# Loading the routing stage's first data during sliding attention, and attention in half blocks

## The reference

```python
def sb_attend(q, k, v, q_pos, k_pos):                      # stick-breaking attention, 8 heads x 64
    z = einsum(q, k) / 8
    mask = k_pos[None, :] < q_pos[:, None]
    log_rest = where(mask, log_sigmoid(-z), 0.0)
    suffix = cumsum(log_rest, axis=3, reverse=True) - log_rest
    a = where(mask, exp(log_sigmoid(z) + suffix), 0.0)
    return einsum(a, v)

def reference(...):
    xn = rmsnorm(x, norm1_g)
    qa, ka, va, qb, kb, vb, ga, gb = split(xn @ w_in)      # 4352 columns
    oa = sb_attend(qa, ka, va)
    ob = sliding_window_attention(qb, kb, vb)              # window 128, sinks, relative bias
    x = x + (sigmoid(ga) * (oa @ w_oa) + sigmoid(gb) * (ob @ w_ob)) @ w_o
    x = x + peer(rmsnorm(x, norm2_g))                      # 8 heads: top 16 of 16384 experts each
    return rmsnorm(x, final_g), keys and values
```

## Time and profile before

| | |
|---|---|
| median of three runs | 3539.45 us |
| range of the three runs | 3533.47 to 3540.75 us |
| profiled execution | 3539.31 us |
| its span, first to last instruction | 3537.6 us |
| mean granted TensorE clock | 0.969 |
| busy: TensorE, VectorE, GpSimd, ScalarE | 93%, 75%, 42%, 23% |

### The profile page before, as it was taken

The page is one execution under the profiler, slowest core; times in us unless marked ns, Lnnn a source line. Parts: engine busy times, 40 slices in busy tenths (PEclk is TensorE's granted clock), DMA queues, the critical chain, the costliest instruction groups (busy, mean ns, idle before and its releaser), DMA issues.

```text
span 3537.6 us, 43678 instructions
## 1 busy us (share of the span) xinstructions
PE 3300.8 (93%) x14507; PEld 1960.5 (55%) x14516; DVE 2640.3 (75%) x5015; ACT 800.3 (23%) x1589; POOL 1494.4 (42%) x1116
## 2 busy tenths in 40 slices
PE   9769999986888899999899999999999999999997
PEld 7436789984465667677544444444444444444443
DVE  2555888845468767775699998888888777888888
ACT  3542112215122337675100001000010000100001
POOL 0000388710223778886234443444443433434342
PEclk9989999988999999999899999999999999999998
DMA  8988699956887679889899999999999999999997
GB/s 351 414 340 302 225 406 401 403 180 214 335 303 262 176 193 200 209 165 202 324 416 395 416 382 417 411 404 405 417 389 415 375 391 401 383 406 399 397 416 285
DMA packets 465464, 1196.04 MB, mean 338 GB/s; under 512 B 195672, under 2 KB 257800, under 8 KB 386568
## 3 DMA queue, kind: packets, MB, share of 16 engines
q0 software_dynamic: 149776, 679.68, 50.2%
q1 hardware_dynamic: 183472, 495.29, 37.0%
q10 hardware_dynamic: 132048, 19.01, 3.6%
HBM read 1124.51 MB, written 70.39 MB: 338 GB/s over the span
## 4 chain that ended last, share of the span: by engine, by line
PE 33%; DVE 11%; DMA 3%; issue 3%; POOL 0%; DVEq 0%; ACT 0%; POOLq 0%
PE k_ps L2689 17%; PE k_ps L2675 16%; DVE k_yacc L2439 5%; DVE d_ring L2425 4%; DMA d_ring<-peer_uv,d_idx 3%; DVE k_acc L2439 0%; DMA out_y<-k_acc 0%; DVE d_a L2447 0%; DVE d_qacc L2457 0%; POOL d_ring L2387 0%; DVE e_topi L2477 0%; DVE d_aw L2434 0%; DVE e_top L2472 0%; DVE e_sc L2474 0%; DVE e_ci L2477 0%
## 5 line engine op out<-in xcount | busy, mean ns | idle before, releaser
L2387 POOL DMA_INDIRECT d_ring<-peer_uv,d_idx x512 | 691.1, 1350 | 1004.8 <-DVEq L2441 900.3
L2675 PE MATMUL k_ps<-k_xd,k_ring 128*128 128x512 f32 x2016 | 889.4, 594 | 7.8 <-DMA k_ring<-u_blocks 5.2
L2675 PEld LDWEIGHTS k_ps<-k_xd,k_ring 128*128 128x128 f32 x2016 | 384.2, 191 | 493.1 <-issue 486.3
L2425 DVE SCALAR_TENSOR_TENSOR d_ring<-d_ring,k_xn 128x1024 f32<-128x1024 f32 x512 | 607.5, 1221 | 53.8 <-DMA d_ring<-peer_uv,d_idx 31.4
L1687 POOL DMA_INDIRECT G<-c_cellg,c_cell x256 | 434.3, 1696 | 114.7 <-issue 88.7
L2689 PE MATMUL k_ps<-k_ring,d_a 128*128 128x512 f32 x1024 | 453.0, 595 | 10.8 <-DVE d_a L2447 10.0
L2689 PE MATMUL k_ps<-d_v,d_a 128*128 128x512 f32 x1024 | 451.6, 594 | 2.4 <-DVE d_qacc L2457 2.2
L2439 DVE SCALAR_TENSOR_TENSOR k_acc<-d_ring,d_aw,k_acc 128x1024 f32<-128x1024 f32 x256 | 328.9, 1285 | 45.8 <-DVE k_acc L2439 29.7
L2439 DVE SCALAR_TENSOR_TENSOR k_yacc<-d_ring,d_aw,k_yacc 128x1024 f32<-128x1024 f32 x256 | 328.9, 1285 | 37.0 <-DVE k_yacc L2439 25.4
L2689 PEld LDWEIGHTS k_ps<-k_ring,d_a 128*128 128x128 f32 x1024 | 195.1, 191 | 259.1 <-issue 257.0
L2634 ACT ACTIVATE d_a<-k_ps 128x512 f32<-128x512 f32 x128 | 76.3, 597 | 1140.5 <-PE k_ps L2675 1108.9
(11 more groups left out here) (423 smaller groups left out, 4265.5 us busy)
## 6 DMA issues: line engine op xcount, KB each, us to landing
c_chunk<-wq SPq DMA_DIRECT2D x128, 512.0 KB
k_ring<-u_blocks SPq DMA_DIRECT2D x128, 512.0 KB, 21.1
s_kc<-sb_kT SPq DMA_DIRECT2D x32, 1024.0 KB, 13.7
s_vc<-sb_v SPq DMA_DIRECT2D x32, 1024.0 KB, 11.2
c_chunk<-w_m SPq DMA_DIRECT2D x64, 512.0 KB
k_ring<-v_blocks SPq DMA_DIRECT2D x64, 512.0 KB, 9.5
d_gb<-G SPq DMA_DIRECT2D x32, 1024.0 KB
d_v<-v_blocks SPq DMA_DIRECT2D x64, 512.0 KB
```

The costliest lines, as they stand in the source:

```text
L2387: pool.indirect_dma_start(out=ring[:, b], out_offset=None, in_=a["peer_uv"], in_offset=bass.IndirectOffsetOnAxis(ap=idx8[par][:, b:b + 1], ...
L2425: last = nc.vector.scalar_tensor_tensor(ring[:, b, 0:D], ring[:, b, 0:D], 1.0, xn[T % 2][:], ALU.mult, ALU.mult, accum_out=h[:, bass.ds(co ...
L2675: last = nc.tensor.matmul(ps[:, HB + x % 2, :], ub[j][:, k], xd[:, k].rearrange("p t q -> p (t q)"), start=(k == 0), stop=(k == KC - 1))
```

## The change

- In `project`, `split(4)` is moved ahead of the first 15 fetches, and so each later split ahead of the 15 fetches that it stood behind; `GELU_BLOCK` is 10.
- In `window`, SP issues the routing stage's first loads after its own last load: five tables, q, k and v of tile 0, chunks 0 to 5, the gates of tile 0. They have their own place in SBUF, and semaphores that outlive the block. The four last clears come behind them. The waits for clears and stores at the end of the block are gone.
- In `decide`, these loads are gone from SP's list; the load of `ob` of turn 1 waits for all stores of `obT`, the loads of `w_o`, `g2` and `subk` for the clears and POOL's other stores. POOL's first scatter waits for the clears.
- `front`, `logs` and the products with `negtri` in `rests` work on the two halves of 512 one after the other; `softened` counts halves.
- In turn 1 TensorE projects `ob` before `rests(0, 0)`, not after `values(0, 0)`.

```diff
-    BETWEEN, GELU_BLOCK, WB = 15, 9, 3
+    BETWEEN, GELU_BLOCK, WB = 15, 10, 3
...
                 experts_of()
+                split(4)
                 fetch(0, BETWEEN)
                 weigh()
-                for b in range(4, NBLK):
-                    split(b)
-                    fetch(BETWEEN * (b - 3), BETWEEN * (b - 2))
+                for b in range(5, NBLK + 1):
+                    if b < NBLK:
+                        split(b)
+                    fetch(BETWEEN * (b - 4), BETWEEN * (b - 3))
...
                 sp.wait_ge(pe_b.sem, pe_b.at(NP - 3, "values"))
                 load_v(NP - 1, 1)
+                for dst, src in ((opening.ident, a["ident"]), (opening.mask, a["mask"]), (opening.negtri, a["negtri"]), (opening.iota, a["iota"]), (opening.token, a["token"])):
+                    sp.dma_start(dst[:], src).then_inc(opening.table_in, 16)
+                sp.dma_start(opening.q[0][:], o["qT"][0]).then_inc(opening.q_in, 16)
+                sp.dma_start(opening.k[0][:], o["kT"][0]).then_inc(opening.k_in[0], 16)
+                sp.dma_start(opening.v[0][:].rearrange("p (b e) q -> p b (e q)", b=2), o["v"][:, :, 0, :].rearrange("b p c -> p b c")).then_inc(opening.v_in[0], 16)
+                for n in range(6):
+                    src = a["w_m"][:, 4 + n] if n < 4 else a["w_m"][:, n - 4]
+                    sp.dma_start(opening.chunk[n][:], src).then_inc(opening.chunk_in[n], 16)
+                sp.dma_start(opening.gate[:].rearrange("p a (b c) -> p (a b) c", c=BW), o["gates"][:, :, 0, :].rearrange("b p c -> p b c")).then_inc(opening.gate_in, 16)
                 clear_gates(CLEARED + 48, (P - CLEARED - 48) // 4)
-                sp.wait_ge(zero_st, 4 * (P - CLEARED))
...
-                pool.wait_ge(ob_st, 16 * NP)
-                pool.wait_ge(rows_st, 16 * len(rows))
...
                 def other(i):
                     if i > 1:
                         sp.wait_ge(eaten, MERGE_AT[i - 1] + 4)
+                    else:
+                        sp.wait_ge(software["b_ob_st"], 16 * (NT - 1))
                     sp.dma_start(flat(ob_sb[:]), o["obT"][SEQUENCE[i]]).then_inc(ob_in, 16)
...
                     if i == 1:
+                        sp.wait_ge(software["b_rows_st"], 64)
+                        sp.wait_ge(software["b_zero_st"], 4 * (P - CLEARED))
                         weights((w_o[:], a["w_m"][:, 8:]), (g2[:], bass.AP(a["g2"].tensor, 0, [[0, P], [1, D]])), (subk[:], a["subk"]))
...
                 nc.vector.memset(zero_b[:], 0.0).then_inc(cast, 1)
-                dve.wait_ge(mask_in, 32)
+                dve.wait_ge(mask_in, 80)
...
-                    dve.wait_ge(act_f.sem, act_f.at(p, "ln"))
-                    nc.vector.scalar_tensor_tensor(soft[p % 3], wide(Z[n % 3]), 0.0, soft[p % 3], ALU.max, ALU.add).then_inc(softened, 1)
+                    for par in range(2):
+                        half = soft[p % 3][:, 512 * par:512 * par + 512]
+                        dve.wait_ge(act_f.sem, act_f.at(p, f"ln{par}"))
+                        nc.vector.scalar_tensor_tensor(half, ps[:, Z[n % 3] + par, :], 0.0, half, ALU.max, ALU.add).then_inc(softened, 1)
...
-                    nc.scalar.activation(soft[p % 3], wide(Z[n % 3]), ACT.Abs).then_inc(act_f.sem, 1)
-                    act.wait_ge(act_f.sem, act_f.at(p, "abs"))
-                    nc.scalar.activation(soft[p % 3], soft[p % 3], ACT.Exp, scale=-1.0).then_inc(act_f.sem, 1)
-                    act.wait_ge(act_f.sem, act_f.at(p, "exp"))
-                    nc.scalar.activation(soft[p % 3], soft[p % 3], ACT.Ln, bias=1.0).then_inc(act_f.sem, 1)
+                    for par in range(2):
+                        half = soft[p % 3][:, 512 * par:512 * par + 512]
+                        nc.scalar.activation(half, ps[:, Z[n % 3] + par, :], ACT.Abs).then_inc(act_f.sem, 1)
+                        act.wait_ge(act_f.sem, act_f.at(p, f"abs{par}"))
+                        nc.scalar.activation(half, half, ACT.Exp, scale=-1.0).then_inc(act_f.sem, 1)
+                        act.wait_ge(act_f.sem, act_f.at(p, f"exp{par}"))
+                        nc.scalar.activation(half, half, ACT.Ln, bias=1.0).then_inc(act_f.sem, 1)
...
                     p, z = pair(t, n), Z[n % 3]
-                    pe.wait_ge(softened, p + 1)
                     for par in range(2):
+                        pe.wait_ge(softened, 2 * p + par + 1)
                         last = nc.tensor.matmul(ps[:, z + par, :], negtri[:], soft[p % 3][:, 512 * par:512 * par + 512], start=False, stop=(n == 0), skip_group_check=True)
...
                 scores(0, 0)
-                pe.wait_ge(tabs, 64)
...
+                    if i == 1:
+                        pe.wait_ge(ob_in, 16)
+                        project(MERGE_AT[1], 6, ob_sb)
                     for n in range(t + 1):
                         rests(t, n)
...
-                    pe.wait_ge(ob_in, 16 * i)
-                    project(MERGE_AT[i], 6, ob_sb)
+                    if i > 1:
+                        pe.wait_ge(ob_in, 16 * i)
+                        project(MERGE_AT[i], 6, ob_sb)
```

More of the change, by code:

```diff
@@ L1176, in project, with window @@
     return used
-def window(nc, a, o, spent, soft, sc, w_m):
+def window(nc, a, o, spent, soft, sc, w_m, opening):
     NP = NT - 1
@@ L1380, in _, with decide @@
                 sums(NP - 1, 1, NP // 2 - 1)
-def decide(nc, a, o, software, acc, aw, row_v, ring, w_o, dense_in, search, ps):
+def decide(nc, a, o, software, acc, aw, row_v, ring, w_o, dense_in, search, ps, opening):
     SEQUENCE = [None] + list(range(NT - 1))
@@ L1413, in decide @@
         sem = lambda n: ctx.enter_context(nc.semaphore(n))
-        chunk = [sb(f"c_chunk{n}", [P, D]) for n in range(NB)]
+        spread = [sb(f"c_spread{n}", [P, P, TS]) for n in range(2)]
+        g2 = sb("c_g2", [P, D])
+        sb("c_opening", [P, OPENING_SIZE // 4])
+        chunk, q_sb, k_sb, v_sb, gate, ident, mask_f, negtri, iota, token, mask_in, q_in, k_in, v_in, gate_in, chunk_in = opening
         subk = sb("c_subk", [P, 2, P])
-        g2 = sb("c_g2", [P, D])
-        ident, negtri, negone = (sb(f"c_{n}", [P, P]) for n in ("ident", "negtri", "negone"))
+        negone = sb("c_negone", [P, P])
         ident_b, mask_b = sb("c_ident_b", [P, P], BF16), sb("c_mask_b", [P, 4, P], BF16)
@@ L1421, in decide @@
         digit = search.digit
-        q_sb, k_sb = [sb(f"c_q{n}", [P, 4, P]) for n in range(2)], [sb(f"c_k{n}", [P, 4, P]) for n in range(3)]
-        v_sb = [sb(f"c_v{n}", [P, 4, P]) for n in range(2)]
         soft = [sb("c_soft", [P, D])[:], ring[:, 6], ring[:, 7]]
@@ L1486, in _ @@
             def _(sp):
-                for dst, src in ((ident[:], a["ident"]), (mask_f, a["mask"])):
-                    sp.dma_start(dst, src).then_inc(mask_in, 16)
-                def tables():
-                    for dst, src in ((negtri[:], a["negtri"]), (digit[:], a["digit"]), (iota[:], a["iota"]), (token[:], a["token"])):
-                        sp.dma_start(dst, src).then_inc(tabs, 16)
                 def query(t):
@@ L1515, in stream @@
                 def stream(first, last):
-                    for n in range(first, last):
-                        if n >= NB:
-                            sp.wait_ge(eaten, n - NB + 1)
+                    for n in range(max(first, NB), last):
+                        sp.wait_ge(eaten, n - NB + 1)
                         kind, x = CHUNKS[n]
@@ L2707, in _ @@
                     values(NG - 1, 1, c, NG // 2 - 1)
+Opening = namedtuple("Opening", "chunk q k v gate ident mask negtri iota token table_in q_in k_in v_in gate_in chunk_in")
 DenseInputs = namedtuple("DenseInputs", "xd xn acc idx gw")
@@ L2749, in build @@
             ps = carried.enter_context(nc.psum_tensor("k_ps", [P, 8, 512], F32))
-            decide(nc, a, o, soft, acc, aw, row_v, ring, w_o, dense_in, search, ps)
+            decide(nc, a, o, soft, acc, aw, row_v, ring, w_o, dense_in, search, ps, opening)
             dense(nc, a, o, soft, acc, ring, dense_in, search, ps)
```

45 lines of the change are left out of this document (26 added, 19 removed).

## The result

The changed kernel takes 3504.69 us (median of four runs, 3501.53 to 3506.62) beside 3539.74 us for the kernel before; the ratio is 0.9903 (95% interval 0.9888 to 0.9919), a gain of about 35 us where 21 were forecast, and 2 us under the low end of the range. The profiled execution has a span of 3503.2 us, 34.4 us less than that of before. So the direction was right and the size was not; the stages show that the 13 us between forecast and result are a sum of misses of both signs.

A forecast was written before the change was run, and what follows sets the result against it. A chain of stages whose durations add up, TensorE nearly always at work, was taken to bound the kernel. The terms -7.7 - 12.0 - 1.5 = -21.2 us on 3539.3 gave 3518 us, own range 3511 to 3523, 8 in 10 3507 to 3530.

The forecast's parts named there:

- two rivals: Projections: TensorE's small "issue" holes grow and 7.7 us is lost (3526, chance 0.12), or they close too (3506, chance 0.12).
- Projections: Projections stage: earlier splits and Gelu one block later close two TensorE holes and spare clock restarts, 4.7 + 3.0 = 7.7 us.
- more from the projections: Projections stage: earlier refills and splits also close TensorE's small "issue" holes, 12 us, time 3506; chance 0.12.
- Dense stage: Dense stage, untouched by the diff: moves as a block with whatever is won or lost earlier.
- Seam and first turn: From sliding attention's end through routing's first turn: 12 us won by early loads, 2.8 of them the seam (6 to 15).
- Turn 2: Routing's second turn: its loads and gathers hang on `y` and `eaten`, so the 12 us are kept.
- Half blocks: Routing's attention by halves: TensorE waits less for VectorE, VectorE's extra adds up, -5.2 + 3.6 = -1.5 us (-5 to +29).
- burden rival: Half-block attention: every pair pays 0.80 us on the path, 36 x 0.80 = 28.9 us, time 3548.5; chance 0.05.

## Why the prediction was right in its direction and wrong in its size

**Base.** The sum was made against one execution, in which block 7 of the projections took 17 us too long. Its row was read (TensorE busy 9.3 of 14 us) and used for two rivals, but not for the question what that lateness covers.

**Projections (-7.7; measured -15.4): a step that failed.** The splits are as forecast: every hole that a split released is gone. What failed is that Gelu one block later "spares ScalarE its wait of 9.50 us, which evictions had slack for (eight banks)": its cover was TensorE's own delay in block 7. Where that is gone TensorE waits 6.9 to 11.9 us near 616 us (four profiles with the old code), and 23.7 us once the splits are early as well; so the edit that was costed at nothing is the one without which the other is worth nothing. TensorE's holes in the stage sum to 13.5 to 17.6 us in the five old executions and to 2.2 to 5.5 in the nine with both edits; the mean granted clock is 0.970 to 0.979 and 0.984 to 0.991. The rival "more from the projections" had a time near the truth, 3506, for a reason that isn't the one (holes that close under full DMA engines).

**Dense stage (0; measured -10.4): the largest miss.** "The dense stage is untouched by the diff, so whatever is won or lost earlier moves it as a block" was wrong; the term was put at nothing without a row. The 36 VectorE instructions that the half blocks add ahead of it change what its branches cost, and a hole of 7 to 8 us of TensorE goes. For the change that is luck: 36 pieces of a memset give it as well.

**Seam and first turn (-12.0; measured -6.8).** Of "With the final waits gone the seam should cost what it costs where nothing is awaited, some 0.3 us" the opposite came: the waits went, and POOL's drain took their place, 6.6 us. The last store lands 6.13 us after its start instead of 2.28; that the opening loads, which are under way at the same time, make it so late is likely (with three of the four clears moved the drain is as long, 6.60 us) but was not tested by itself. The order of work after it came as forecast: products 0.85 us after routing's start, `ob` ahead of `rests`, no wait for chunk 6, and from the first `gates` product to `y` 21.9 us instead of 22.9. `ob`'s projection started 12.0 us after the last store instead of 8.1, and the two projections were 9.1 and 8.8 us long instead of 8.9 and 7.1, with the granted clock at 0.50 (1.2 GHz) until 856.2 and again for 3.4 us from 866.4. In the nine executions with the opening loads and POOL's last store, `ob` starts after 9.8 to 12.1 us, and in six of them the projection of `oa` takes the forecast 7.1. From the last store to `y` 8.9 of the 12 us were won; sliding attention, which the prediction left as it was, took 2.2 us of that.

**Turn 2 (0; measured +3.9).** "The loads and gathers of turn 2 hang on `y` and on `eaten`, so the 12 us are kept" was wrong: the v that is asked for behind `y`'s store lands 11.6 us after its issue at 900.69, TensorE waits 6.2 us for it instead of 1.5, and behind that hole the clock is at its lower level: the projection of `ob` takes 8.8 us instead of 7.1. The half blocks have a part in it, which bring TensorE to this v sooner; with them alone the turn takes 93.8 us.

**Half blocks (-1.5; measured -2.3 in turns 3 to 8).** The mechanism was right: TensorE's waits for VectorE fell from 25.0 to 16.1 us in 15 instead of 17 waits; the mean of the eight profiles with whole blocks is 21.4 (20.0 to 25.0) and of the ten with half blocks 15.7 (13.7 to 17.0). The size agrees, but 2.3 us is hardly more than the spread of the means, and the sum left out turn 2, where the one profile of the half blocks alone is 3 us longer. The burden rival (0.80 us on each of 36 pairs) is refuted: of the turns from 3 to 8 only turn 3 grew by more than 0.2 us on the mean, by 0.9.

So -7.7 and -10.4 us were missed on one side, and +5.2 and +3.9 on the other, and it is luck that the forecast came as near as it did.

## What to carry to other kernels

An edit costed at nothing needs its cover named with the time at which it holds: here a wait of 9.5 us was hidden by a delay that another edit of the same change removed, and that a second execution did not even have. Take two profiles of before when a sum rests on rows of one stage. A wait at the end of a block that is taken out may be made again by the drain of the engine that issued the last transfer, so read who closes the block; and time won or lost in a stage that no edit touches is to be looked for where its loops branch, since 36 small instructions far ahead were worth 8.5 us. A wait that is made shorter can be given back at the next one, as in turn 2, where the longer hole brought the lower clock with it.

## What the runs showed of the hardware that was not expected

- VectorE pays for some branches back to a loop's head: 10 to 11 us, or 5 to 6 us, or 0.5, always the same branches for the same instruction count (18 profiles). The Trainium skill, "Runtime: NRT & Kernel Launch", section "Instruction fetch mechanics", says that a taken branch whose target is outside the window held forces a transfer of the target page before execution goes on. The trace agrees: each costly branch has an instruction transfer 2.8 to 4.1 us behind it, two lie in a gap of 10 us, and a branch that costs 0.5 us has none within 11 us. Why the same loop pays on some turns and not on others stays open.
- TensorE's stretches of "issue" holes in the first profile of before (425 to 429, 521 to 527 and 546 to 553 us) let through some four products with their weight loads every 1.43 us. They came in one of the five executions with the same code for this stage, and their cause stays open.
- POOL's drain at the end of a block lasts 6.6 us after its last store where other transfers are under way, and 1.04 us where the store had been awaited; SP's lasts 0.12 us from 844.5 us, and its last clear lands at 851.3.
